# Three of eight experts with 64 slots and two weight streams, experts 1 to 7 sorted by token count, in a two-layer decoder trunk

## The reference

```python
logits = h @ w_router                       # 256 tokens, 8 experts
top_vals, top_idx = top_k(logits, 2)
combine = one_hot(top_idx) weighted by softmax(top_vals)
y = 0
for e in range(8):                          # w_gate, w_up: 1024 x 1408; w_down: 1408 x 1024
    y += combine[:, e] * ((silu(h @ w_gate[e]) * (h @ w_up[e])) @ w_down[e])
```

## Time and profile before

| | us |
|---|---|
| median of three runs | 1055.9 (1055.19 to 1056.5) |
| the profiled execution | 1055.26 |
| its span, first to last instruction | 1053.2 |
| PE, DVE, ACT, POOL busy in it | 1040.3, 835.4, 678.7, 144.8 |
| mean granted TensorE clock | 0.998 |

### The profile page before, as it was taken

One profiled execution on the slowest core, in us unless ns is written; L12 is line 12 of the kernel. 1 busy time (PEld: TensorE's weight loads), 2 busy tenths in 40 slices (PEclk: granted clock), 3 DMA queues, 4 the chain that ended last, 5 costly groups with the idle time before them and its releaser, 6 DMA issues.

```text
span 1053.2 us, 15497 instructions
## 1 busy us (share of the span) xinstructions
PE 1040.3 (99%) x5669; PEld 848.2 (81%) x5669; DVE 835.4 (79%) x1164; ACT 678.7 (64%) x971; POOL 144.8 (14%) x177
## 2 busy tenths in 40 slices
PE   8999999999999999999999999999999999999997
PEld 7988888888888888999887878777777777676775
DVE  6879776988666766687967797898898889889885
ACT  7776746556443534676665555877777777777784
POOL 5004332001100000000613000450101010101011
PEclk9999999999999999999999999999999999999999
DMA  9553544567456546363444548799999999999993
GB/s 285 196 163 113 172 128 158 162 230 272 147 209 230 170 140 195 102 221 120 127 164 142 175 143 290 258 388 343 320 357 391 371 333 389 370 388 366 390 378 100
DMA packets 131282, 252.74 MB, mean 240 GB/s; under 512 B 6606, under 2 KB 56868, under 8 KB 131204
## 3 DMA queue, kind: packets, MB, share of 16 engines
q1 hardware_dynamic: 129444, 245.93, 67.0%
q0 software_dynamic: 1296, 4.20, 1.9%
q10 hardware_dynamic: 464, 1.58, 0.4%
HBM read 247.49 MB, written 4.19 MB: 239 GB/s over the span
## 4 chain that ended last, share of the span: by engine, by line
PE 92%; DVE 5%; ACT 1%; issue 1%; DMA 1%; POOL 0%; SPq 0%; DVEq 0%; POOLq 0%; ACTq 0%
PE PS L826 28%; PE PS L1367 12%; PE PS L1369 12%; PE PS L1368 12%; PE PS L1231 8%; PE PS L1232 4%; PE PS L1178 2%; PE PS L1180 2%; PE PS L1179 2%; PE PS L850 2%; DVE m_lo L2223 2%; PE PS L1038 1%; PE PS L1322 1%; DVE scr L2531 1%; DVE big L2523 1%
## 5 line engine op out<-in xcount | busy, mean ns | idle before, releaser
L517 DVE TENSOR_TENSOR w_lo<-ring,w_hi 128x1536 fp32r<-128x1536 f32 (+1 forms) x190 | 304.5, 1618 | 80.0 <-ACT w_hi L504 79.3
L504 ACT ACTIVATE w_hi<-ring 128x1536 fp32r<-128x1536 f32 (+1 forms) x191 | 260.4, 1369 | 99.3 <-PE PS L1232 47.8
L1667 ACT ACTIVATE m_hi<-ring 128x512 fp32r<-128x512 f32 (+2 forms) x256 | 157.8, 632 | 119.7 <-PE PS L826 117.9
L2223 DVE TENSOR_TENSOR m_lo<-ring,m_hi 128x512 fp32r<-128x512 f32 (+2 forms) x256 | 182.3, 743 | 58.3 <-ACT m_hi L1667 56.3
L826 PE MATMUL PS<-m_hi,h_both 128*128 128x512 f32 (+3 forms) x640 | 178.5, 365 | 0.7 <-DVE m_lo L2223 0.6
L826 PEld LDWEIGHTS PS<-m_hi,h_both 128*128 128x128 f32 x640 | 113.0, 188 | 19.9 <-DVE m_lo L2223 2.5
L1231 PE MATMUL PS<-h_both,w_hi 128*128 128x512 f32 x352 | 124.4, 398 | 0.0
L826 PE MATMUL PS<-m_lo,h_both 128*128 128x512 f32 (+3 forms) x320 | 115.0, 359 | 0.0
L1367 PE MATMUL PS<-w_hi,hTe 128*96 128x512 f32 (+1 forms) x288 | 108.8, 378 | 0.0
L1369 PE MATMUL PS<-w_lo,hTe 128*96 128x512 f32 (+1 forms) x288 | 108.1, 375 | 0.0
L1368 PE MATMUL PS<-w_hi,hTe 128*96 128x512 f32 (+1 forms) x288 | 107.7, 374 | 0.0
(11 more groups left out here) (386 smaller groups left out, 1976.1 us busy)
## 6 DMA issues: line engine op xcount, KB each, us to landing
ring<-in_w_in_dram SPq DMA_DIRECT2D x39, 1024.0 KB, 5.2
ring<-in_w_exp_gate_dram SPq DMA_DIRECT2D x48, 768.0 KB, 8.2
ring<-in_w_exp_up_dram SPq DMA_DIRECT2D x48, 768.0 KB, 8.0
ring<-in_w_exp_down_dram SPq DMA_DIRECT2D x24, 1536.0 KB, 8.9
ring<-in_w_branch_dram SPq DMA_DIRECT2D x12, 1024.0 KB, 5.1
ring<-in_w_ffn_gate_dram SPq DMA_DIRECT2D x12, 768.0 KB, 5.5
ring<-in_w_ffn_up_dram SPq DMA_DIRECT2D x12, 768.0 KB, 5.4
ring<-in_w_ffn_down_dram SPq DMA_DIRECT2D x6, 1536.0 KB, 6.3
```

Source lines behind the costliest of these rows:

```text
L504: act.activation(split_parts(u, j)[0], ring[:, i % NSLOT, w0:w0 + words], ACT.Copy)\
L517: dve.tensor_tensor(lo, ring[:, (j // 2) % NSLOT, w0:w0 + words], hi.bitcast(F32), SUB).then_inc(sem(f"lo_ready{b}"), 1)
L1667: act.activation(hi, raw, ACT.Copy).then_inc(sem("m_hi_ready"), 1)
L2223: dve.tensor_tensor(lo, raw, hi.bitcast(F32), SUB).then_inc(sem("m_lo_ready"), 1)
```

## The change

Experts 1 to 7 are handled in an order that the kernel finds out: it counts tokens (`expert_counts` on PE), ranks the experts on DVE (`sorted_places`), and moves all routing tables from "by expert" to "by place". Expert 0 keeps place 0. The three with the fewest tokens take the places 2, 4 and 6 (`SMALL`). SP reads the expert at each place from `order` and loads its weights; its loop is unrolled.

A small place has 64 slots. The 64 hi and 64 lo columns of its tokens stand side by side as one stationary operand of 128 columns, so that w_hi and w_lo each stream past once (`two`): rows 0 to 63 of the result hold the x_hi sums and rows 64 to 127 the x_lo sums. These two halves must then be added: ACT copies the bank to `folds`, and PE adds the lower half onto the upper one with a matmul by `shift`. There are eight such folds for each small place: gate and up of three groups, and the two banks of D, which are folded during the next expert.

The gather batches become place 0, places 1 to 3 (now inside place 0) and places 4 to 7 (inside place 3). A small place that got more than 64 tokens, or another with more than 96, would start a second pass.

```diff
-CAP = 96
-PASSES = -(-T // CAP)
+CAP, FEW = 96, 64
+SMALL = (2, 4, 6)
+PASSES = -(-T // FEW)
...
+FEW_AFTER = {2: [("fold", 0)], 4: [("folded", 0)], 5: [("fold", 1)], 7: [("folded", 1), ("gu", 0)], 8: [("fold", 2)],
+             9: [("tr", 0)], 10: [("folded", 2)], 11: [("fold", 3)], 13: [("folded", 3), ("gu", 1)],
+             15: [("tr", 1), ("fold", 4)], 16: [("tr", 2), ("folded", 4)], 17: [("fold", 5)],
+             18: [("folded", 5), ("gu", 2)], 20: [("tr", 3)]}
+FOLDS, DOWN_FOLDS = 8, (6, 7)
...
-BATCHES = [(0, 2), (2, 3), (5, 3)]
-BATCH_IN = {1: 1, 3: 2}
-BATCH_AFTER = {j: k for k, j in enumerate((6, 7, 9, 10, 12, 13, 16, 18))}
+BATCHES = [(0, 1), (1, 3), (4, 4)]
+BATCH_IN = {0: 1, 3: 2}
+BATCH_AFTER = {0: {j: k for k, j in enumerate((9, 10, 12, 13, 15, 16, 18, 19))},
+               3: {j: k for k, j in enumerate((6, 7, 9, 10, 12, 13, 16, 18))}}
 TSLOTS = 5
+PREVIOUS_FOLDED, PREVIOUS_ROWS = 2, 6
+TSLOT = (0, 1, 2, 4, 0, 1, 2, 3)
...
+    if e in BATCH_IN and j in BATCH_AFTER[e]:
+        what.append(("gather", BATCH_AFTER[e][j]))
+    if e - 1 in SMALL and j == PREVIOUS_FOLDED:
+        what.append(("rows_folded", 0))
...
+RANK_AT = [0] + [0] * (NE - 1)
+for _i, _e in enumerate(SMALL + tuple(e for e in range(1, NE) if e not in SMALL)):
+    RANK_AT[_e] = _i + 1
...
+def slots_of(e):
+    return FEW if e in SMALL else CAP
...
-            with sp.Fori(1, NE) as e:
-                expert_loads(eg, eu, ed, e, e)
+
+            def expert_in(e):
+                return sp.value_load(order[0:1, e:e + 1], min_val=0, max_val=NE - 1)
+
+            sp.wait_ge(sem("routing_known"), ROUTING_KNOWN["order_known"])
+            for e in range(1, NE):
+                expert_loads(eg, eu, ed, expert_in(e), e)
...
+            def expert_counts():
+
+                for a in range(TT):
+                    mm = pe.matmul(totals, ones[:, :], msel[:, a, :], start=(a == 0), stop=(a == TT - 1))
+                mm.then_inc(sem("totals_full"), 1)
+
+            def folded(r, e, i):
+
+                pe.wait_ge(sem("fold_full"), fold_no(r, e, i) + 1)
+                bank, n = fold_of(i)
+                pe.matmul(PS[:, bank, 0:n], shift[:, :, :], folds[:, i % 2, 0:n], start=False, stop=True,
+                          skip_group_check=True).then_inc(sem("folded"), 1)
...
-                if isinstance(r, int):
-                    for a in range(TT):
-                        mm = pe.matmul(totals, ones[:, :], msel[:, a, :], start=(a == 0), stop=(a == TT - 1))
-                    mm.then_inc(sem("totals_full"), 1)
...
+                def two(dst, x, whi, wlo, start, stop):
+                    pe.matmul(dst, x, whi, start=start, stop=False)
+                    return pe.matmul(dst, x, wlo, start=False, stop=stop)
 
                 def last_down(n, j):
 
@@ -1388,7 +1473,8 @@
                 for batch, (e0, _) in enumerate(BATCHES):
                     if e == e0 and batch:
                         gathered(batch, KD - 1)
-                hTe_hi, hTe_lo = hTe[:, e % TSLOTS, 0, :, :], hTe[:, e % TSLOTS, 1, :, :]
+                hTe_hi, hTe_lo = hTe[:, TSLOT[e], 0, :, :], hTe[:, TSLOT[e], 1, :, :]
+                hTe_few = few_tokens(e)
...
+                            pe.wait_ge(sem("routing_known"), ROUTING_KNOWN["order_known"])
...
+                            if e in SMALL:
+                                mm = two(PS[:, 6 + c, :], hdT_few[:, t, :, :], hi[:, w], lo[:, w], t == 0, t == FT - 1)
+                                continue
...
+                            if e in SMALL:
+                                mm = two(PS[:, 2 * (g % 2) + up, 0:gn * P], hTe_few[:, kt, :, :], hi[:, k, :], lo[:, k, :],
+                                         kt == 0, kt == KD - 1)
+                                continue
...
-                    if e == 0 and j == 3:
+                    if e == 0 and j == 0 and isinstance(r, int):
+                        first_gathered(r, KD // 2)
+                        expert_counts()
+                    if e == 0 and j == 4:
                         row_scales(r)
                     for what, x in expert_after(e, j):
+                        if what == "folded":
+                            folded(r, e, x)
+                        elif what == "rows_folded":
+                            for i in DOWN_FOLDS:
+                                folded(r, e - 1, i)
...
+                runs = slot_runs(batch)
+                for run in runs:
+                    s0, c0, n = TSLOT[run[0]], (run[0] - e0) * CAP, len(run)
+                    if run[0] in SMALL:
+                        ins = act.activation(few_tokens(run[0])[:, k, 0, :], PS[:, 4 + b, c0:c0 + FEW], ACT.Copy)
+                    else:
+                        ins = act.activation(hTe[:, s0:s0 + n, 0, k:k + 1, :],
...
+            def fold(r, e, n, i):
+
+                bank, words = fold_of(i)
+                x = fold_no(r, e, i)
+                wait_used(act, expert_unit(n), fold_after(i))
+                if isinstance(x, int) and x == 0:
+                    act.wait_ge(sem("residual_out"), 16 * TT)
+                    for half in range(2):
+                        act.activation(shift[:, half, :], ident[:, (1 - half) * FEW:(2 - half) * FEW], ACT.Copy)
+                if not isinstance(x, int) or x > 1:
+                    act.wait_ge(sem("folded"), x - 1)
+                act.activation(folds[:, i % 2, 0:words], PS[:, bank, 0:words], ACT.Copy).then_inc(sem("fold_full"), 1)
...
+                    if j == ESPLIT - 1 and e - 1 in SMALL:
+                        for i in DOWN_FOLDS:
+                            fold(r, e - 1, n - 1, i)
+                    if e > 0 and j == (PREVIOUS_ROWS if e - 1 in SMALL else ESPLIT - 1):
                         rows_out(r, e - 1, n - 1)
                     for what, g in expert_after(e, j - ESPLIT):
-                        if what == "gu":
+                        if what == "fold":
+                            fold(r, e, n, g)
...
+            def sorted_places():
+
+                dve.wait_ge(sem("totals_full"), 1)
+                dve.wait_ge(sem("constants"), 1 + HALF + 3 + 1)
+                step(dve.tensor_copy(counts, PS[:, LOGIT_BANKS[1], NE:2 * NE]))
+                step(dve.tensor_tensor(key, counts, key_off, ADD))
+                step(dve.tensor_tensor(smaller, key.unsqueeze(1).broadcast_to([P, NE, NE]), key.unsqueeze(2).broadcast_to([P, NE, NE]),
+                                       ALU.is_lt))
+                step(dve.tensor_reduce(size_rank, smaller, AX.X, ADD))
+                step(dve.tensor_tensor(moves, size_rank.unsqueeze(1).broadcast_to([P, NE, NE]),
+                                       rank_at.unsqueeze(2).broadcast_to([P, NE, NE]), ALU.is_equal))
+                step(dve.tensor_tensor(mixed, by_expert.unsqueeze(2).broadcast_to([P, 8, NE, NE]),
+                                       moves.unsqueeze(1).broadcast_to([P, 8, NE, NE]), MUL))
+                step(dve.tensor_reduce(by_place, mixed, AX.X, ADD))
+                dve.tensor_copy(order[:, 1:NE], expert_at[:, 1:NE]).then_inc(sem("routing_known"), 1)
...
+                    sorted_places()
                     most_rows()
+                where = pos_placed if isinstance(r, int) else pos_left
```

167 lines of the change are left out of this document (113 added, 54 removed).

## The result

The changed kernel takes 1068.8 us (median of four runs, 1067.6 to 1072.9) against 1055.7 for the kernel before on the same chip: 1.3% slower, ratio 1.013 with a 95% interval of 1.0102 to 1.0158. The prediction, 1049.7 with a range of 1044 to 1056.5, was wrong in sign, by 19.1 us. The profiled execution took 1072.9 us with a span of 1071.2. It lies 4.2 above the median, so what is counted up from its trace is a little more than the median shows.

A forecast was written before the change was run, and what follows sets the result against it. PE was taken to lead, with DVE and the weight transfers right behind. Terms -12.45 + 3.1 + 1.4 + 1.4 + 1.0 = -5.55 us on a 1053.2 span gave 1047.65, plus 2.06: 1049.7 us, range 1044 to 1056.5.

The forecast's parts named there:

- the 1.0 that was allowed for transfers: From expert 4 on: the stream needs 184 us for four experts, PE wants 180, stock covers about 4; +1.0 us.
- What the change removes: Small experts at places 2, 4 and 6: 42.7 us each instead of 46.85, with DVE limiting; -12.45 us.
- The first rival: Expert stage: transfers are the bound already at 378 GB/s, six experts take 281.4 us, total 1054.5; chance 0.20.
- What it adds at the start: Start of expert 0: the sort delays piece 4 by 1.8 us and row scales cost 1.3; +3.1 us.
- Row scales: Start of expert 0: behind piece 4 they no longer fill a PE gap and cost 1.3 us.
- The wait for the token totals: Start of expert 0: token totals behind piece 0 add 0.2 us where PE waits anyway; DVE's wait was unpriced.
- The copies of gathered tokens are half as wide and end about 0.5 sooner: Before the sort at expert 0's start: narrower copies let the sort begin about 0.5 us sooner.
- The first batch moves from expert 1 into expert 0 at the same price: Gather of three experts, now in place 0: costs the same 4.2 us as in expert 1.
- Gathers of four: Second gather batch, in place 3: four experts, 384 columns, 5.6 us instead of 4.2; +1.4 us.
- folds of D: In the expert after each small one: two 512-column matmuls, 3 x 0.46; +1.4 us.
- No second pass: Whole kernel: token counts fit the slots; the rival of a second pass, over 360 us more, had chance 0.02.
- Folds are not passed on to DVE: Small experts: the rival that folds delay DVE said 47.3 us each, total 1062.5; chance 0.13.

The follow-up runs named there:

- e8: The changed kernel, with each up-weight piece of places 2, 4 and 6 loading only its first slice of 128 rows (those outputs are others): 1060.1 us.
- e13: e7 with the reduced up-weight loads of e8 in places 2, 4 and 6 (those outputs are others): 1048.4 us.
- e11: The kernel before, with the reduced up-weight loads of e8 and SP's expert loop unrolled (those outputs are others): 1055.9 us.
- e7: e6 plus two 384-column matmuls on zeros ahead of every piece that continues a bank in places 2, 4 and 6: 1058.4 us.
- e12: e6 with the reduced up-weight loads of e8 in places 2, 4 and 6 (those outputs are others): 1053.8 us.
- e10: The kernel before, with eight more DVE instructions of the sort's shapes ahead of the router's values, results unused: 1059.7 us.
- e9: The kernel before, with the first gather's matmuls 96 columns wide instead of 192 (expert 1's output is another): 1058.4 us.
- e5: e2 plus the gather of experts 1 to 3 moved to other pieces of place 0, away from the shared PSUM bank: 1063.3 us.
- e2: The changed kernel, with DVE computing the router's values before the sort instead of after it: 1065.5 us.
- e6: e5 plus the first gather 192 columns wide (second half unused) and 4 matmuls on zeros ahead of piece 4: 1060.4 us.
- e4: The changed kernel without the 24 folds, neither ACT's copies nor PE's matmuls (small experts' outputs are others): 1066.9 us.

## Why the prediction was wrong, by its steps

On the profiled executions the miss is 1071.2 - 1047.65 = 23.5 us: the first expert matmul 1.5 later, place 0 12.4, the three small places 10.2, the tail behind the experts 0.5, less the 1.0 that was allowed for transfers. The other four places add nothing.

**"What the change removes", -12.45: the step that failed most.** The three places took 138.3 us instead of 128.1. The working (PE 32.8, DVE 41.7, ACT 40 to 41.6, so 42.7) was right for the three engines: e8 and e13 measure 41.3 to 43.3. What stood in its place is the transfers first, and the clock with them. The prediction wrote that the stream needs 45.3 to 46.9 us for an expert and then charged it as +1.0 us for the last four, in the belief that a rate between 378 and 392 GB/s would hold and that a stock covers the rest. Whole small places got 365 to 380, and the last four took 185.0 us where PE wanted 180. For place 2 it charged nothing, and that place has half of the miss, 5.0 us. The row for it was there: at the 369 GB/s of this expert before, 17.75 MB take 48.1 us, and it took 47.7. e8 and e11 together show that the bytes are the cause: the same bytes are worth 8.7 us after the change and nothing before. The first rival had the right mechanism and 0.20 of the chance, but its price was low as well. Its 281.4 us for six experts are 285.8 here (777.8 to 1063.6), and 283.7 in e7, where the clock holds better.

The bytes alone do not make up the whole miss. Over all profiles of versions with folds, small places with all their bytes and no half clock took 43.1 to 45.9 us (seven of them), and those with 6.8 us at half clock 45.4 to 48.0 (seven). With fewer bytes it is 41.3 to 42.2 (four) and 44.2 to 45.2 (two, in e12, with 6.1 and 6.8 us at half). So each of the two is worth 2 to 3 us in a small place. The stops with which the clock fell are these, here in place 4:

```profile
909.93 0.69 PE L1432 MATMUL PS<-folds,shift 128*128 128x384 f32 x1 [2.07 <-ACT folds L2149]
...
920.75 0.76 PE L1453 MATMUL PS<-w_hi,hdT_few 128*128 128x512 f32 x1 [2.38 <-DVE hdT_few L2907]
```

Place 2 has the same two (2.35 and 2.36 us), each with 3.4 us at 0.50; place 6 has them too (1.48 and 2.27) and stayed at 1.00. PE, with less to do, stands there for ACT's copy and for DVE. Whether late weights make these stops longer was not shown; that e8 has half as much half clock in the small places fits it.

That a core streaming alone gets about 425 GB/s is what the Trainium skill says ("HBM Reference", "Specifications (TRN2)"). No place here shows it: the highest over a whole place is 388 (e7, place 5). An expert of 17.75 MB would take 41.8 us at 425, an estimate from the page's figure, and then the predicted 42.7 would have stood; by measurement it stands at 46. Single slices of 1.2 us come near the page's figure, up to 426 in place 2, and fall to 191 in the same place.

**"What it adds at the start", +3.1: mis-sized.** The duration of the sort was right (2.8 us), its effect was not. e10 puts it alone at +4.0 by the medians; in its profiled execution place 0 is 5.1 longer, 2.4 of them delay, where 1.8 was said, and 2.7 from the half clock behind the stop. In the changed kernel the first gather and the bank stop come on top, and 16.9 us of place 0 are at half clock. At 1.5 to 1.6 us for each 3.4, as in the four windows under e13, an estimate of some 8 of the 12.4 us missing in place 0 is the clock; the two bank stops (3.8 us) and the later piece 4 would be the rest. Row scales, priced at 1.3 from a row at full clock, took 2.4 in the changed kernel at half clock (676.9 to 679.3 in the chain of waits). The wait for the token totals ahead of the sort, priced at nothing, was 0.73.

**"The copies of gathered tokens are half as wide and end about 0.5 sooner": wrong in sign.** They are narrower, but PE's gather before them is too, the clock fell at 657.4, and place 0 began 1.5 us later instead of 0.5 sooner. e9 shows it alone: +2.7 us. The fall is frequent and not certain: e5 has the same gather and kept 1.00.

**"The first batch moves from expert 1 into expert 0 at the same price": wrong.** The 4.2 us are right, but the new positions (behind pieces 15 and 19) meet a transposition in the same PSUM bank. e5 removes the stop; its gain of 2.2 us over e2 lies within the spread of the runs. The order of the bank's uses was in the code, and the price of waiting for it could have been read from DVE's queue there.

**The clock as a whole.** No term and no rival had it, since all rows of before show 1.00. What the rows here show is that where PE stops for some 2 us, or has only narrow matmuls, the granted clock often falls to 0.50 (1.2 GHz) for 3.4 to 10.3 us behind it, and that it may or may not do so for the same stop: 1.9 us ahead of piece 4 went with no half clock in e12, and with 3.4 us at 0.50 in e6, 6.9 in e7 and 10.2 in e13. The Trainium skill ("TensorE: Matmul & The Clock Gate", "A second HAM failure mode: psum-queue depth-cycling") says that short idle times between groups of matmuls as PE goes round the PSUM banks can make the clock fall and rise again and again, and that this is paid in the bursts between. The stretch at 708.6 to 712.0 agrees in part: a wait for a bank, then 0.50, but it is one wait of 2.54 us and not many short ones.

**What was right.** Gathers of four, +1.4, and folds of D, +1.4: places 3, 5 and 7 took 53.0, 47.3 and 47.1, where 52.9, 47.3 and 47.3 were said. No second pass. Folds are not passed on to DVE (e4). The test named in advance, "wrong if a small expert takes over 45 us, or the start costs over 6", caught both: two of three take over 45, and place 0 costs 70.0 - 50.2 - 4.2 = 15.6.

**What stays open.** Which stop takes the clock with it was not settled: e12 and e13 have the same code in place 0 and differ there by 4.7 us. Nor was it settled how much of the small places' half clock is a consequence of the waits for weights. Nor was it tried whether the sort on another engine than DVE would leave place 0 at its 54.4 us (50.2 and the gather).

## What to carry to other kernels

When an engine leads by a few per cent, look for the resource right behind it and give the gain only up to there: 17.75 MB at the rate of a whole expert was 46.9 us, PE's expert 46.85, so no more than the stock was to be had. Take the rate of the very stage that is to get shorter, since it can differ from one to the next (369 in expert 2, 378 in expert 5). Halving the work of a matmul that keeps PE busy, or putting a dependent chain of 2.8 us ahead of a split, can cost more than the work itself, as the granted clock can fall there (e9, e10): read it in every window first. When a block of PE work is moved, list which bank it takes and who frees that bank there.

## What was not expected of the hardware

A gather with half the columns (96 instead of 192) took 4.0 us instead of 2.3, because the clock was 0.50 in it (e9); in e5, at 1.00, it took 2.3. Added matmuls on zeros made a kernel faster: 34 more in each of three places brought 5.4 us where the transfers were short (e13 against e12, whose profiles have 125.4 and 132.0 us in these places), and 2.0 with all bytes, within the spread (e7 against e6). A load queue that is full delivered 365 to 380 GB/s over the small places whether or not PE waited for it, against 369 to 378 before, though 392 had stood over 15 us.
